# Narrow matmul rows split up: modulation sums in two parts, a token panel laid between MoBA's scores, zero matmuls at the first norm

## What is computed

```python
# first block: modulation from c, used by both norms and both residual gates
mod = (silu(c) @ w_mod + b_mod)                 # 6 x 1024 values
sh1, sc1, g1, sh2, sc2, g2 = split(mod, 6)
h = rms_norm(x) * (1 + sc1) + sh1
proj = h @ w_in
... y_a = sgu_branch(u, v, ...); y_b = ssd_branch(z, xbc, dt, ...)
x = x + g1 * (mixed @ w_out)
h2 = rms_norm(x) * (1 + sc2) + sh2
x = x + g2 * (square(relu(h2 @ w_ff1)) @ w_ff2)
# second block
proj = rms_norm_2(x, attn_g) @ w_in_2
y_moba = moba_attention(rope(mq), rope(mk), mv)  # 8 heads of 64, causal softmax over 256 keys
og = gla_attention(gq, gk, gv, log_a)            # 4 heads, then a norm per head
og = og * rsqrt(mean(og * og) + eps) * gla_norm_g
x = x + concat([y_moba, og * silu(gr)]) @ w_out_2
x = x + (silu(conv(h_gate)) * conv(h_val)) @ w_ffn_down
return rms_norm_2(x, final_g)
```

## Time and profile before

| | |
|---|---|
| time, median of 3 runs | 938.48 us (936.16 to 939.41) |
| profiled execution | 940.62 us, of which span 938.9 us |
| PE busy | 922.6 us, 98% of the span |
| DVE / ACT busy | 717.1 us (76%) / 546.7 us (58%) |
| mean granted TensorE clock | 0.992 |

### The profile page before, as it was taken

How to read it: one execution, slowest core, us unless ns; L and a number is a source line. 1 busy time by engine, 2 the same in 40 slices (tenths; PEclk the granted TensorE clock), 3 DMA queues, 4 the chain that set the end, 5 groups by cost and what they waited for, 6 DMA issues and landing times.

```text
span 938.9 us, 17275 instructions
## 1 busy us (share of the span) xinstructions
PE 922.6 (98%) x6692; PEld 849.0 (90%) x6692; DVE 717.1 (76%) x963; ACT 546.7 (58%) x760; POOL 117.2 (12%) x95
## 2 busy tenths in 40 slices
PE   8999999999999999999999999999999999999997
PEld 4799999999898989988888888999878999999885
DVE  4947788899999968568877556679876798877664
ACT  4366656666676575355655445567665676666442
POOL 0000200044744400010000001303100100000000
PEclk8999999999999999999999999999999999999999
DMA  9954555568767756645656565535433355655661
GB/s 337 360 183 136 180 179 181 182 226 245 222 221 234 244 192 208 191 140 159 201 184 196 185 197 181 164 109 189 134 103 112 113 182 198 189 187 184 194 210 45
DMA packets 85709, 175.53 MB, mean 187 GB/s; under 512 B 5441, under 2 KB 46801, under 8 KB 85649
## 3 DMA queue, kind: packets, MB, share of 16 engines
q1 hardware_dynamic: 84672, 172.39, 56.7%
q0 software_dynamic: 368, 1.31, 0.4%
q10 hardware_dynamic: 608, 1.00, 0.3%
HBM read 173.63 MB, written 1.05 MB: 186 GB/s over the span
## 4 chain that ended last, share of the span: by engine, by line
PE 81%; DVE 9%; DMA 4%; issue 3%; ACT 1%; DVEq 0%; SPq 0%; ACTq 0%
PE proj_ps L1651 17%; PE proj_ps L1634 14%; PE proj_ps L1635 14%; PE proj_ps L1636 14%; PE proj_ps L1654 9%; DVE mod_acc L952 5%; DMA raw<-in_panels 3%; DVE w_lo L940 2%; PE proj_ps L1694 1%; PE proj_ps L1695 1%; PE proj_ps L1696 1%; PE aux L2009 1%; PE aux L1722 1%; DMA mod_first<-in_panels 1%; PE aux L1730 1%
## 5 line engine op out<-in xcount | busy, mean ns | idle before, releaser
L940 DVE TENSOR_TENSOR w_lo<-raw,w_hi 128x1024 fp32r<-128x1024 f32 x276 | 347.8, 1273 | 126.8 <-ACT w_hi L473 126.1
L473 ACT CAST w_hi<-raw 128x1024 fp32r<-128x1024 f32 x276 | 286.6, 1047 | 196.6 <-PE proj_ps L1636 72.5
L1634 PE MATMUL proj_ps<-act_pair,w_hi 128*128 128x256 f32 x1024 | 292.3, 285 | 0.4 <-issue 0.4
L1635 PE MATMUL proj_ps<-act_pair,w_hi 128*128 128x256 f32 x1024 | 289.6, 283 | 0.0
L1636 PE MATMUL proj_ps<-act_pair,w_lo 128*128 128x256 f32 x1024 | 289.6, 283 | 0.0
L1634 PEld LDWEIGHTS proj_ps<-act_pair,w_hi 128*128 128x128 f32 x1024 | 196.2, 192 | 4.8 <-issue 2.7
L1635 PEld LDWEIGHTS proj_ps<-act_pair,w_hi 128*128 128x128 f32 x1024 | 196.3, 192 | 0.6
L1636 PEld LDWEIGHTS proj_ps<-act_pair,w_lo 128*128 128x128 f32 x1024 | 196.3, 192 | 0.0
L1651 PE MATMUL proj_ps<-act_pair,w_hi 128*128 128x512 f32 x256 | 69.9, 394 | 0.0
L1651 PE MATMUL proj_ps<-ff_pair,w_hi 128*128 128x512 f32 x256 | 69.9, 394 | 0.0
L437 POOL TENSOR_TENSOR tmp_b<-tmp_b 128x512 f32<-128x512 f32 x4 | 5.2, 1297 | 465.2 <-ACT tmp_b L496 465.2
(11 more groups left out here) (337 smaller groups left out, 1631.5 us busy)
## 6 DMA issues: line engine op xcount, KB each, us to landing
raw<-in_panels SPq DMA_DIRECT2D x308, 512.0 KB, 4.0
mod_first<-in_panels SPq DMA_DIRECT2D x16, 512.0 KB, 10.8
xres<-in_x_t SPq DMA_DIRECT2D x2, 512.0 KB, 6.0
out_t<-tmp_a SPq DMA_DIRECT2D x4, 256.0 KB, 2.2
wst<-in_ws_t POOLq DMA_DIRECT2D x1, 512.0 KB, 3.8
bs_sb<-in_bs_rows POOLq DMA_DIRECT2D x1, 512.0 KB, 4.5
level_sb<-in_levels ACTq DMA_DIRECT2D x1, 512.0 KB, 5.5
cols<-in_cols SPq DMA_DIRECT2D x1, 267.0 KB, 3.2
```

The source lines that it names most:

```text
L473: nc.scalar.copy(w_hi[:, s, :], raw[:, s, :]).then_inc(hi_done, 1)
L940: tt(out=w_lo[:, s, :], in0=raw[:, s, :], in1=w_hi[:, s, :].bitcast(F32), op=ALU.subtract).then_inc(taken, 1)
L1634: mm(dst, hi, xh, start=first and k == 0 and nt % 2 == 0, stop=False, skip_group_check=True)
L1635: mm(dst, hi, xl, start=False, stop=False, skip_group_check=True)
```

## The change

Three edits on PE's program alone; no other engine's program is altered.

1. At the first norm one zero matmul (`keep_warm(1, 0)`, into bank 0) is put before the wait on `mod_acc_ok` and one between the two halves of `mod_sum`.
2. In the SSD stage each `mod_sum` is cut: column tiles 0 to 3 stay where they were, tiles 4 to 7 go behind the first twelve matmuls of the next group's `zg_panel(0)` (after the last group: of the first `gm` panel). `mod_mm` is counted after the second part.
3. In the second block the third token panel of chunk `i2 + 5` no longer stands behind `moba_scores(2)` and `moba_turn(1)`: its token tile 0 goes before the scores and its tile 1 between the scores and the turn.

```diff
-            def token_panel(g, s, par, k0, first=False, last=False):
+            def token_panel(g, s, par, k0, first=False, last=False, tiles=range(TT)):
                 pe.wait_ge(taken, landed_group(g) * SLOTS + (s + 1))
-                for t in range(TT):
+                for t in tiles:
...
-                ins.then_inc(used, 1)
+                if TT - 1 in tiles:
+                    ins.then_inc(used, 1)
...
-            def mod_sum(cols_ps, first=True):
-                for nt, dst in enumerate(cols_ps):
-                    ins = mm(dst, mod_acc[:, nt * P:nt * P + P], ones[:, 0:1], start=first, stop=True, skip_group_check=not first)
-                ins.then_inc(S["mod_mm"], 1)
+            def mod_sum(cols_ps, first=True, nts=range(8)):
+                for nt in nts:
+                    ins = mm(cols_ps[nt], mod_acc[:, nt * P:nt * P + P], ones[:, 0:1], start=first, stop=True, skip_group_check=not first)
+                if 7 in nts:
+                    ins.then_inc(S["mod_mm"], 1)
...
                     if (half, n) == (0, N_HALF - 1):
+                        keep_warm(1, 0)
                         pe.wait_ge(S["mod_acc_ok"], 2 * KT - PE_MOD)
-                        mod_sum(first_cols(1))
+                        mod_sum(first_cols(1), nts=range(4))
+                        keep_warm(1, 0)
+                        mod_sum(first_cols(1), nts=range(4, 8))
...
-                zg_panel(0)
+                if par == 0 and not first:
+                    zg_panel(0, release=0, nts=(0, 1))
+                    mod_sum(ssd_cols, nts=range(4, 8))
+                    zg_panel(0, nts=(2, 3))
+                else:
+                    zg_panel(0)
...
-                    mod_sum([aux[:, 3, n:n + 1] for n in range(8)])
+                    mod_sum(ssd_cols, nts=range(4))
...
-                panel(GROUP["gm"] + 1, s, 1, ya_hi, ya_lo, 2 * s, s == 0, s == SLOTS - 1)
                 if s == 0:
+                    panel(GROUP["gm"] + 1, s, 1, ya_hi, ya_lo, 2 * s, True, release=0, nts=(0, 1))
+                    mod_sum(ssd_cols, nts=range(4, 8))
+                    panel(GROUP["gm"] + 1, s, 1, ya_hi, ya_lo, 2 * s, True, nts=(2, 3))
                     group_sum(7)
+                else:
+                    panel(GROUP["gm"] + 1, s, 1, ya_hi, ya_lo, 2 * s, False, s == SLOTS - 1)
...
+            token_panel(i2 + 5, 2, 1, 4, tiles=(0,))
             moba_scores(2)
+            token_panel(i2 + 5, 2, 1, 4, tiles=(1,))
             moba_turn(1)
-
-            token_panel(i2 + 5, 2, 1, 4)
             pe.wait_ge(S["og_diag"], 1)
```

More of the change, by code:

```diff
@@ L1717, in row_of, with keep_warm @@
                 mm(aux[:, 3, 0:T], ones[:], flat(diag[:]), start=True, stop=True).then_inc(S["rs_mm"], 1)
-            def mod_sum(cols_ps, first=True):
-                for nt, dst in enumerate(cols_ps):
-                    ins = mm(dst, mod_acc[:, nt * P:nt * P + P], ones[:, 0:1], start=first, stop=True, skip_group_check=not first)
-                ins.then_inc(S["mod_mm"], 1)
+            def mod_sum(cols_ps, first=True, nts=range(8)):
[3 more added lines that the diff above has]
+                    ins.then_inc(S["mod_mm"], 1)
             def first_cols(half):
                 return [aux[:, 1, n:n + 1] for a in (0, 8) for n in range(a + 4 * half, a + 4 * half + 4)]
-            def keep_warm(n):
+            def keep_warm(n, bank=3):
                 for _ in range(n):
-                    mm(aux[:, 3], ones[:], warm[:], start=True, stop=True)
+                    mm(aux[:, bank], ones[:], warm[:], start=True, stop=True)
             pe.wait_ge(S["ready"], N_READY)
@@ L1821, in group_sum @@
                 ins.then_inc(S["gs_mm"], 1)
+            ssd_cols = [aux[:, 3, n:n + 1] for n in range(8)]
             def ssd(g, par, mod, first=False, last=False):
                 x_hi, x_lo = (ya_hi, ya_lo) if last else (act_hi, act_lo)
-                zg_panel = lambda s: panel(g + (GROUP["zg"] + 1), s, 1 - par, x_hi, x_lo, 2 * s, s == 0, s == SLOTS - 1,
-                                           g * 2 + (zg0 + 1))
+                zg_panel = lambda s, **kw: panel(g + (GROUP["zg"] + 1), s, 1 - par, x_hi, x_lo, 2 * s, s == 0, s == SLOTS - 1,
+                                                 g * 2 + (zg0 + 1), **kw)
                 x, b, c_t = stg[:, par, 0:2], stg[:, par, 2], stg[:, par, 3]
```

## The result

The changed kernel takes 940.42 us (median of 22 runs, 938.75 to 942.12), the kernel before 938.08 us (22 runs, 936.16 to 940.12). The ratio is 1.0025, 95% interval 1.0018 to 1.0032: about 2.3 us slower. The interval lies above 1, so there is a loss, though it is smaller than the 0.3% that the prediction took as the least that counts. The forecast time was 941.0 us. The ratios in this document are not quotients of the two medians beside them; the two can differ by half a us, and readings rest on the ratio and its interval.

The account below looks back on a forecast made before the run. PE, busy 98%, was taken as the bound, with its waits and low-clock stretches. Against the profile: 940.62 - 0.3 + 0.1 + 0.9 = 941.3; from the median, 941.7 without falls, about 940.4 with one; taken 941.0, range 937.0 to 943.0.

Parts of the forecast that it names:

- MoBA, the main term: Second block: the later turn delays copy, exponentials, GLA scaling and output panel; +0.9 us, or +2.3 without the earlier fall.
- rival B: Second block: as A, and the new 2.8 us wait makes the clock fall in most executions; 942.6 us, chance 0.2.
- First norm: First norm: zero matmuls avoid the clock's fall but DVE gets the sum later; -0.3 us, +0.8 had the clock stayed up.
- SSD: SSD stage: cutting the sums adds wide-narrow changes, mostly hidden by PE's waits; +0.1 us, from -1.0 to +0.6.
- The late evacuation: SSD stage: `mod_mm` comes 1.5 us of panel later, hidden but for about 0.25 us at the last group.
- A: Whole kernel, the sum: the chain from turn to GLA scaling replaces the clock as output panel's hold; 940.0 to 941.9, chance 0.45.
- Rival C: Second block: copy doesn't hold the exponentials, or turn comes earlier; falls simply gone; 937.2 us, at most 935.5, chance 0.15.

Follow-up runs that it names:

- e2: The third edit alone on the kernel before; 941.29 us against 938.69, ratio 1.0029.
- e10: DVE's GLA scaling ahead of the normalisation of unit 2, alone on the kernel before; 938.20 us against 937.37, ratio 1.0010.
- e3: The changed kernel with the turn of unit 1 moved ahead of the scores; 937.04 us against 938.69 before, ratio 0.9983.
- e4: The changed kernel with DVE's GLA scaling ahead of the normalisation of unit 2; 937.62 us against 938.69 before, ratio 0.9984.
- e11: The changed kernel with ACT's exponentials of unit 2 ahead of the copy of the turn; 936.55 us against 937.37 before, ratio 0.9994.
- e8: The kernel before with only the third edit, reordered as tile 0, turn, scores, tile 1; 937.58 us against 937.87, ratio 0.9997.
- e1: The changed kernel with its third edit undone, the other two kept; 938.70 us against 938.69 before, ratio 0.9999.
- e6: The first edit alone (zero matmuls and cut at the first norm) on the kernel before; 937.91 us against 937.87, ratio 0.9999.
- e5: The changed kernel with two unused 128x512 matmuls in PE's wait before the output panel; 938.38 us against 937.87 before, ratio 1.0010.
- e9: The changed kernel with both the turn ahead of the scores and DVE's GLA scaling ahead of the normalisation; 937.19 us against 937.37 before, ratio 1.0002.
- e7: The second edit alone (cut sums in the SSD stage) on the kernel before; 937.81 us against 937.87, ratio 1.0001.

## Why the prediction was right, step by step

All stretches together, in us; the columns are the same as above.

| profiles | first norm | stretch of the second block |
|---|---|---|
| order of before, clock falls | 13.02, 12.99, 13.15 (14.63 with a double fall) | 15.68, 15.66 |
| order of before, clock stays | 11.48 | 14.11, 14.11, 14.12 |
| zero matmuls and cut (8 profiles) | 12.34 to 12.86 | |
| third edit as changed | | 16.28, 16.29, 16.29 |
| third edit with one or two repairs | | 14.31 to 14.42 |

The 13.15 is that of e2 and holds 0.21 us in which DVE waited for a load. The 11.48 is a single profile (e10).

**MoBA, the main term.** The chain was right: turn, copy, table load, exponentials, normalisation, GLA scaling. It was tried at three of its links, each alone: the turn (e3), DVE's order (e4), ACT's order (e11). Each takes back 1.9 to 2.0 us of the stretch, while taking back the other two edits (e2) takes back nothing of it. Its size was put at +0.9 us against an execution with the fall and +2.3 without; the runs show 16.28 - 15.68 = +0.6 and 16.28 - 14.11 = +2.2. The copy came 2.23 us later, as against 2.3 forecast. The 0.3 us of difference lie half there and in the handing on to the scaling, which starts at 700.49 while the normalisation drains until 700.57, and half on ACT: `mix_hi` and V's evacuation start 1.90 us apart (703.44 and 705.34), before 2.04 (705.03 and 707.07). The wait was forecast at 2.8 us and is 2.48, short by the same.

**How often the clock fell.** Outside the start, the last few us and the places named here, no profile shows a stretch at the lower clock. One stretch of 3.4 us at half the clock lowers the mean over a kernel of 938.6 us by 3.4 / 2 / 938.6 = 0.0018. The mean granted clock is on record for the 22 runs of the changed kernel and for all runs of the experiments, those of the kernel before beside them included. Averaged over the runs of each kernel it is:

| first norm | second block | kernels | runs | mean granted clock |
|---|---|---|---|---|
| as before | as before | before | 99 | 0.9932 |
| as before | turn early | e8 | 12 | 0.9935 |
| as before | new wait | e2 | 12 | 0.9913 |
| zero matmuls | as before | e1, e6 | 24 | 0.9955 |
| zero matmuls | new wait | changed | 22 | 0.9938 |
| zero matmuls | wait filled | e5 | 12 | 0.9959 |
| zero matmuls | repaired | e3, e4, e9, e11 | 48 | 0.9959 |

What follows from this is an estimate. The start has one or two such stretches in the profiles, which puts some 0.2 to 0.3 of a stretch of noise on a mean over twelve runs; the kernel before has 0.9927, 0.9933 and 0.9936 in its three sets of runs; and the clock of a run doesn't say where it fell. The new wait takes 0.0021 (0.9959 - 0.9938) with the zero matmuls and 0.0022 (0.9935 - 0.9913) without them, so about one stretch per execution. The first norm of before takes 0.0024 (0.9959 - 0.9935), 1.3 stretches, in keeping with its profiles: four of five fell there, one of them for two stretches on end. The row of narrow matmuls in the second block takes 0.0003 to 0.0004, a fall in one execution of five and hardly above the noise; two of its five profiles have one.

**The fall behind the wait** was kept out of the sum, as rival B with a price of 1.6 us. In the profiles it is there in one of two without a filling, at 1.47 us; by the granted clocks it is there in most executions, as B said. PE's waits in the SSD stage, up to 1.4 us, brought none in thirteen profiles.

**First norm.** Forecast -0.3 us against an execution with the fall, +0.8 without. The profiles show 12.79 - 13.02 = -0.2, and +0.9 to +1.4 against 11.48. The two falls had been priced at 1.1 and 1.4 us; they cost 13.02 - 11.48 = 1.5 and 15.68 - 14.11 = 1.6. DVE's step came 6.89 us behind its L952 instead of 6.23, so 0.66 later and not 0.8. If the kernel before falls there about 1.3 times per execution, the edit should gain: 12.6 us on average over the eight profiles with it, against 11.48 + 1.3 * 1.5 = 13.4, so about -0.8 us. This is an estimate; e6 found -0.1, from -1.5 to +1.2. Against an execution without the fall it is a loss.

**SSD.** Forecast +0.1, from -1.0 to +0.6. Its run says 0.0, plus or minus 1.2. The stage took 149.6 to 152.9 us in the eight profiles with the cuts (mean 150.9) and 151.2 to 153.2 in the five without (mean 152.1). That would be a gain of 1.1 us, of the size of the spread, and no stretch at the lower clock was seen there in any of the thirteen profiles. PE's waits for the decay matrices differ: 2.8 us before, 2.0 in the changed kernel, 1.5 in e7. The late evacuation was forecast to cost 0.25 us at the last group; DVE waits 0.17 us for the sum there and nowhere else in the stage. Whether the cuts help by something stays open.

**The median.** The forecast was 941.0 against 938.48, a loss of 2.5 us, made of +0.8, +0.1 and +2.3 for executions without falls, less something for those with one. The loss of about 2.3 us is put together otherwise. The estimates from the rows above are: the stretch of the second block 16.28 against 14.11 + 0.2 * 1.6 = 14.4, so +1.9; the fall behind the wait once per execution, +1.5; the first norm -0.8; the SSD stage 0 to -1.1. That adds up to +1.5 to +2.6. So the mechanism of the main term was right, while the fall behind the wait, which the sum left out, and the gain at the first norm, which it took for a loss, each move the sum by more than 1 us, in opposite directions. That the number came so near is in this part luck. B was right on the clock and 2.2 us too high in its time (942.6); it had taken over the loss at the first norm from A.

**Rival C** asked for ACT's copy before 698.1 in the time of before, thus within 5.6 us behind the start of the mean squares. It came 6.49 us behind. Its picture fits the stretch of the repaired kernels: there the falls are gone, no new wait stands, and the stretch is 1.3 us shorter than before with a fall. Its gain of 1.3 us over the median fits e3 and e4 but was not found in e9.

**A faster version.** e3 and e4 measured 0.9983 and 0.9984, e8, e9 and e11 0.9997, 1.0002 and 0.9994. The profiles explain a modest size: in the stretch the repaired orders take 14.31 to 14.42 us, against 15.68 with the fall and 14.11 without. They gain 1.3 us where the kernel before falls and lose 0.2 to 0.3 where it doesn't, which by the granted clocks is more often. What is left of a gain in e3, e4, e9 and e11, which keep all the edits, can as well come from the first norm. The intervals of e3 and e4 lie below 1, those of the other three hold it. A version that beats the kernel before by more than about 1 us is not shown.

## What to carry to other kernels

A row of narrow work that lets the clock fall costs about 1.5 us, and only in those executions in which it falls; moving a small producer behind wide work delays all that is queued behind its consumers in every execution. Before laying wide matmuls between narrow ones, look for the narrow result that another engine has first in its queue, and keep that one ahead. A wait that this makes on TensorE can cost a fall of the clock on top. And compare one order with the clock up and down at the same place, and see from the granted clocks of many runs how often it falls there, before paying matmuls to hold it up.

## What the runs showed of the hardware

A fall to 1.2 GHz cost 1.5 to 1.6 us (13.02 - 11.48, 15.68 - 14.11, 221.77 - 220.30), and the one that went on for two stretches in e7 3.1 us (14.63 - 11.48 = 3.15). The same program fell at a place in one execution and not in the next: at the first norm 13.02 with the fall and 11.48 without, in the second block 15.68 and 14.11. Two idle matmuls in the wait kept it up: the mean granted clock over the runs of e5 was 0.9959, that of the changed kernel 0.9938. PE's wait of 2.48 us was followed by a fall in one profile (changed) and not in the other (e2). Outside the start, the SSD stage, and these places, stretches of 140 to 350 us repeated to within a few hundredths to a few tenths of a us from kernel to kernel. The cost of one place in such a part can then be read from one profile, though the time of the whole kernel moves by 4 us.
